# Expert lists of a routed MoE: rows of a table in memory, loaded for each step, in place of one-hot matmuls from the fourth expert on

## What is computed

```python
def hier_moe(h, w_rg, b_rg, w_re, b_re, w_gate, w_up, w_down):
    x = h.reshape(-1, D)
    gprob = softmax(x @ w_rg + b_rg)              # 4 groups, the best one is taken
    gp, gidx = top_k(gprob, 1)
    elog_sel = (x @ w_re + b_re), the 4 of the group
    ep, eidx = top_k(softmax(elog_sel), 2)        # 2 of its 4 experts
    ep = ep / sum(ep)
    weights = gp * ep
    # for each of the 16 experts, with c its weight for each token (0 for most):
    y = (silu(x @ wg) * (x @ wu)) @ wd            # 1024 -> 512 -> 1024
    acc = acc + c[:, None] * y
x = x + hier_moe(rmsnorm(x));  output rmsnorm(x)
```

## Time and profile before

| what | value |
|---|---|
| median of 3 runs | 881.52 us |
| the profiled execution | 881.83 us |
| its span | 880.0 us, so 1.8 us lie around it |
| TensorE busy | 846.6 us (96%) |
| VectorE, ScalarE, GpSimd busy | 525.6, 376.2, 251.2 us (60%, 43%, 29%) |
| experts (block 3) | from 431 us to the end |
| TensorE's clock in the steps | 1.00 of full speed |
| DMA in the steps | 0.79 to 0.94 of the 16 engines' time, about 300 GB/s |

### The profile page before, as it was taken

The page is one execution under the profiler, slowest core; times in us unless marked ns, Lnnn a source line. Parts: engine busy times, 40 slices in busy tenths (PEclk is TensorE's granted clock), DMA queues, the critical chain, the costliest instruction groups (busy, mean ns, idle before and its releaser), DMA issues.

```text
span 880.0 us, 15697 instructions
## 1 busy us (share of the span) xinstructions
PE 846.6 (96%) x5784; PEld 748.8 (85%) x5784; DVE 525.6 (60%) x1211; ACT 376.2 (43%) x710; POOL 251.2 (29%) x272
## 2 busy tenths in 40 slices
PE   4999999999999999999899999999999999999993
PEld 3999878999988887776699988899988999888892
DVE  5526424566778435456675576666666655765673
ACT  7445302645357524544335433344343454333542
POOL 1000000000000020001145655546554556453662
PEclk9999999999999899998599999999999999999997
DMA  9220101102222092436278889888799888899771
GB/s 297 59 96 10 39 1 48 49 1 56 49 96 96 13 294 74 177 140 226 70 249 302 291 292 355 279 307 299 282 317 335 296 290 283 286 365 308 257 252 58
DMA packets 117609, 167.08 MB, mean 190 GB/s; under 512 B 15988, under 2 KB 94904, under 8 KB 117573
## 3 DMA queue, kind: packets, MB, share of 16 engines
q1 hardware_dynamic: 102213, 136.00, 45.8%
q0 software_dynamic: 15360, 30.59, 10.1%
HBM read 147.36 MB, written 41.17 MB: 214 GB/s over the span
## 4 chain that ended last, share of the span: by engine, by line
PE 40%; POOL 3%; issue 3%; DVE 2%; DMA 1%; ACT 1%; POOLq 0%; DVEq 0%; ACTq 0%
PE bank L1891 26%; PE bank L1901 3%; PE bank L1912 3%; PE bank L1903 3%; PE bank L1902 3%; PE bank L1879 1%; DMA out<-ot,lists_now 1%; POOL out L1799 1%; POOL hold_at L1815 1%; PE bank L1872 1%; DVE wdlo L2095 1%; ACT split L1991 0%; POOL big L1786 0%; POOL sums L1799 0%; PE bank L1884 0%
## 5 line engine op out<-in xcount | busy, mean ns | idle before, releaser
L1891 PE MATMUL bank<-big,ring 128*128 128x160 f32 x2048 | 285.1, 300 | 1.4 <-DVE x L2167 1.3
L1891 PEld LDWEIGHTS bank<-big,ring 128*128 128x128 f32 x2048 | 280.8, 190 | 2.8 <-DVE x L2167 1.4
L1815 POOL TENSOR_TENSOR hold_at<-ident 128x1 f32<-128x1 f32 x63 | 55.1, 875 | 167.1 <-DVE lists L2062 120.7
L2095 DVE TENSOR_TENSOR wdlo<-wdn,split 128x1024 fp32r<-128x1024 f32 x64 | 76.7, 1218 | 0.0
L1991 ACT CAST split<-wdn 128x1024 fp32r<-128x1024 f32 x64 | 64.9, 1039 | 0.0
L1987 ACT ACTIVATE sg<-bank 128x160 f32<-128x160 f32 x64 | 19.4, 304 | 105.9 <-PE bank L1891 105.7
L499 PE MATMUL bank<-split,ring_r 128*128 128x384 f32 (+1 forms) x192 | 64.5, 336 | 0.1
L501 PE MATMUL bank<-split,ring_r 128*128 128x384 f32 (+1 forms) x192 | 61.7, 321 | 0.0
L1901 PE MATMUL bank<-split,hs 128*128 128x512 f32 x128 | 52.6, 411 | 0.0
L2090 DVE TENSOR_TENSOR hs<-hid,hs 128x128 fp32r<-128x128 f32 x64 | 18.8, 293 | 56.5 <-ACT hs L1993 56.5
L1378 PE MATMUL bank<-split,ring_r 128*128 128x512 f32 (+1 forms) x128 | 51.7, 404 | 0.3 <-PEq L1170 0.3
(11 more groups left out here) (386 smaller groups left out, 1821.2 us busy)
## 6 DMA issues: line engine op xcount, KB each, us to landing
wdn<-in_w_down SPq DMA_DIRECT2D x32, 1024.0 KB, 9.4
ring<-in_w_gate SPq DMA_DIRECT2D x32, 1024.0 KB, 6.0
ring<-in_w_up SPq DMA_DIRECT2D x32, 1024.0 KB, 9.5
ring<-in_w_in SPq DMA_DIRECT2D x8, 1024.0 KB, 6.2
x<-in_x_prompt SPq DMA_DIRECT2D x8, 512.0 KB, 5.9
h_rows<-h SPq DMA_DIRECT2D x8, 512.0 KB, 2.6
sums<-x SPq DMA_DIRECT2D x8, 512.0 KB, 3.7
v<-in_x_prompt SPq DMA_DIRECT2D x4, 512.0 KB, 6.9
```

The lines of the kernel that those rows point to most:

```text
L1815: nc.gpsimd.tensor_tensor(hold_at[:], ident[:, 0:1], ident[:, 1:2], ALU.add).then_inc(e_hold, 1)
L1891: x = nc.tensor.matmul(bank[f % 2][:, side * 256:side * 256 + W], ring[:, u, k, c0:c0 + P], xT[:, k, :], start=k == 0, stop=k == KC - 1)
L2095: nc.vector.tensor_tensor(wdlo[:, k, :], wdn[:, k // 2, (k % 2) * D:(k % 2 + 1) * D], wdhi[:, k, :].bitcast(F32), ALU.subtract).then_inc(e ...
```

## The change

From the fourth expert on the lists are no longer made by one-hot products. Block 3 works out, once, for each token and each of its two experts the row number in a table `records` in DRAM (18304 rows of 8 float32, 32 bytes; row = group start + rank), writes a record of the four list entries and the weight, and sends the records there with 18 indirect DMAs of 128 rows each. In each step SyncE loads the 160 rows of a later step's group with five DMAs, and three VectorE instructions make lists and weights of them. The lists of experts 0 to 2 are still made the old way. Block 2 fills the table with blank records first, and makes `table` for three experts only.

```diff
+        nc.gpsimd.memset(blank[:], 0.0).then_inc(r_gc, 1)
...
+        sp.wait_ge(r_gc, GC + 7)
+        sp.dma_start(places.records.rearrange("(p r) c -> p (r c)", p=P), blank[:].rearrange("p r c -> p (r c)")
+                     ).then_inc(s_states, 16)
...
         for part in (2, 3, 4):
-            link(nc.vector.tensor_copy(table[:, :, :, part], rest))
+            link(nc.vector.tensor_copy(table[:, 0:3, :, part], rest))
...
@@ SyncE, block 3, at the end of each loop pass
+            sp.wait_ge(e_sent, 16 * 2 * TT)
+            sp.wait_ge(e_idx, i + 3)
+            group_rows = places.records[0:GROUPS * W, :].rearrange("(s r) c -> s r c", r=W)[bass.ds(i + 3, 1), :, :]
+            sp.dma_start(listed[:, 0, :], group_rows[:, 0:P, :].rearrange("o r c -> (o r) c")).then_inc(e_list, 16)
+            for j in range(4):
+                sp.dma_start(listed[j * W2:(j + 1) * W2, 1, :], group_rows[:, P:W, :].rearrange("o r c -> (o r) c")
+                             ).then_inc(e_list, 16)
...
@@ GpSimd, block 3, between the first rows_old and the loop
+        pool.wait_ge(e_record, 1)
+        for a in range(2):
+            for t in range(TT):
+                nc.gpsimd.indirect_dma_start(
+                    out=places.records, in_=record[:, a, t, :], in_offset=None, bounds_check=GROUPS * W - 1,
+                    out_offset=bass.IndirectOffsetOnAxis(ap=row_at[:, a, t:t + 1], axis=0),
+                    oob_is_err=False).then_inc(e_sent, 16)
...
@@ TensorE, step
             if not last:
-                pe.wait_ge(e_oh, i + 3)
-                pe.wait_ge(e_idx, i + 2)
-                indices(facts)
+                if first:
+                    pe.wait_ge(e_oh, 3)
+                    pe.wait_ge(e_idx, 2)
+                    indices(table[:, 2, :, :])
                 pe.wait_ge(e_xg, i * 16 + 32)
...
@@ VectorE, block 3
+        def places_of():
+            ranks = rank_m[:].rearrange("p (e t) -> p t e", e=NE)
+            for a in range(2):
+                m = weighing.picks[:, a, :, :]
+                nc.vector.tensor_tensor(chosen[:, a, :, :], m, ranks, ALU.mult)
...
+        def records_of():
+            token = places.token[:].unsqueeze(1).broadcast_to([P, 2, TT])
+            link(nc.vector.tensor_tensor(second[:, 0, :], group[:, 3, :], group[:, 2, :], ALU.is_lt))
...
+        def next_list(i):
+
+            dve.wait_ge(e_list, i * 80)
+            nc.vector.tensor_copy(lists[:, :, 0], listed[:, 0, 0:4])
+            nc.vector.tensor_copy(weight[:], listed[:, :, 4])
+            nc.vector.scalar_tensor_tensor(out=lists[:, :, 1], in0=listed[:, 1, 0:4], scalar=4.0,
+                                           in1=chunk[:].broadcast_to([P, 4]), op0=ALU.mult, op1=ALU.add).then_inc(e_idx, 1)
+        places_of()
...
         def third_table():
-            dve.wait_ge(e_rk, 2)
             onehot(2)
-            dve.wait_ge(e_oh, 3)
-            lower(2)
+            records_of()
             dve.wait_ge(e_g, 80)
...
@@ VectorE, step
-                dve.wait_ge(e_ix, i + 3)
-                indices(i + 2)
-                dve.wait_ge(e_rk, i + 3)
-                onehot((i + 3) % NE)
-                dve.wait_ge(e_oh, i + 4)
-                lower((i + 3) % NE)
+                if first:
+                    dve.wait_ge(e_ix, 3)
+                    indices(2)
+                else:
+                    next_list(i)
```

More of the change, by code:

```diff
@@ L57 @@
 ROUNDS = -(-N // W)
+GROUPS = NE * ROUNDS + 2
+FIELDS = 8
+RUN = -(-GROUPS * W // P)
+OUTSIDE = float(1 << 18)
 class Weighing:
@@ L98, in state_products_out, with __init__ @@
     x.then_inc(signal, 1)
+class Places:
+    def __init__(self, sb, records):
+        self.start = sb("group_start", [P, NE])
+        self.limit = sb("round_limit", [P, ROUNDS - 1])
+        self.token = sb("token", [P, TT])
+        self.outside = sb("outside", [P, TT])
+        self.records = records
 class Halves:
@@ L134, in program @@
     sums_dram = nc.dram_tensor("sums", [N, D], F32).ap()
+    records = nc.dram_tensor("records", [RUN * P, FIELDS], F32).ap()
     with ExitStack() as whole:
@@ L188, in program @@
         lists0 = sb("lists0", [P, 2], I32)
+        places = Places(sb, records)
         s_w = [sem(f"s_w{j}") for j in range(5)]
@@ L1174, in b2_all @@
 def b2_all(nc, A, O, S0, Sp, s_w, samples, halves, sb, sem, e_w, wdn, bank, ident, onesf, eps_c, uT, gT, ring, x1, x_rows, h2_dram,
-           sums_dram, rank_m, table, iota_w, steps, once, weighing, rows_0):
+           sums_dram, rank_m, table, iota_w, steps, once, weighing, rows_0, places):
     c2 = ExitStack()
@@ L1196, in b2_all @@
     later = sb("later", [P, TT, 4], ctx=c2)
+    blank = sb("blank", [P, RUN, FIELDS], ctx=c2)
     both = sb("both", [P, TT, 4], ctx=c2)
@@ L1255, in _ @@
                        allow_small_or_imprecise_dtypes=True).then_inc(r_gc, 1)
+        nc.gpsimd.memset(blank[:], 0.0).then_inc(r_gc, 1)
+        nc.gpsimd.iota(places.start[:], [[W, NE]], base=0, channel_multiplier=0,
+                       allow_small_or_imprecise_dtypes=True).then_inc(r_gc, 1)
+        nc.gpsimd.iota(places.limit[:], [[W, ROUNDS - 1]], base=W, channel_multiplier=0,
+                       allow_small_or_imprecise_dtypes=True).then_inc(r_gc, 1)
+        nc.gpsimd.iota(places.token[:], [[P, TT]], base=0, channel_multiplier=1,
+                       allow_small_or_imprecise_dtypes=True).then_inc(r_gc, 1)
+        nc.gpsimd.memset(places.outside[:], 0.0).then_inc(r_gc, 1)
+        pool.wait_ge(r_gc, GC + 5)
+        nc.gpsimd.memset(blank[:, :, 1:4], FAR).then_inc(r_gc, 1)
+        pool.wait_ge(r_gc, GC + 6)
+        nc.gpsimd.memset(places.outside[NS:P, TT - 1:TT], OUTSIDE).then_inc(r_gc, 1)
+        pool.wait_ge(r_gc, GC + 7)
         for p in range(2):
@@ L1694, in b3_all @@
 def b3_all(nc, A, O, S0, samples, sb, sem, e_w, ring, wdn, bank, ident, eps_c, rows, h2_dram, sums_dram, rank_m, table, iota_w, steps,
-           once, weighing, rows_0):
+           once, weighing, rows_0, places):
     c3 = ExitStack()
     xg, xg2, xT, oh, wdhi, chunk = rows_0.xg, rows_0.xg2, rows_0.xT, rows_0.oh, rows_0.wdhi, rows_0.chunk
-    facts = sb("facts", [P, TT, PARTS], BF16, ctx=c3)
+    chosen = sb("chosen", [P, 4, TT, NE], ctx=c3)
+    group = sb("group", [P, 4, TT], ctx=c3)
+    past = sb("past", [P, 2, TT, ROUNDS - 1], ctx=c3)
+    row = sb("row", [P, 2, TT], ctx=c3)
+    row_at = sb("row_at", [P, 2, TT], I32, ctx=c3)
+    second = sb("second", [P, 2, TT], ctx=c3)
+    inside = sb("inside", [P, 2, TT], ctx=c3)
+    record = sb("record", [P, 2, TT, FIELDS], ctx=c3)
+    listed = sb("listed", [P, 2, FIELDS], ctx=c3)
     far = sb("far", [P, 2], ctx=c3)
@@ L1934, in step @@
                     pe.wait_ge(e_idx, 1)
-                    indices(facts)
+                    indices(table[:, 1, :, :])
                 if f == 0 and not first:
@@ L2068, in _, with link, picked @@
         dve.sem_inc(e_z, 1)
-        lower(0)
+        chain = [0]
+        def link(ins):
+            chain[0] += 1
+            ins.then_inc(e_d, 1)
+            dve.wait_ge(e_d, chain[0])
+        def picked(a, field):
+            return record[:, a, :, field]
+        def places_of():
[3 more added lines that the diff above has]
+                nc.vector.tensor_tensor(chosen[:, a, :, :], m, ranks, ALU.mult)
+                x = nc.vector.tensor_tensor(chosen[:, 2 + a, :, :], m, places.start[:].unsqueeze(1).broadcast_to([P, TT, NE]),
+                                            ALU.mult)
+            link(x)
+            link(nc.vector.tensor_reduce(group[:], chosen[:], axis=AX.X, op=ALU.add))
+            link(nc.vector.tensor_tensor(past[:], group[:, 0:2, :].unsqueeze(3).broadcast_to([P, 2, TT, ROUNDS - 1]),
+                                         places.limit[:].unsqueeze(1).unsqueeze(1).broadcast_to([P, 2, TT, ROUNDS - 1]),
+                                         ALU.is_ge))
+            link(nc.vector.tensor_reduce(row[:], past[:], axis=AX.X, op=ALU.add))
+            link(nc.vector.scalar_tensor_tensor(out=row[:], in0=row[:], scalar=float((NE - 1) * W), in1=group[:, 0:2, :],
+                                                op0=ALU.mult, op1=ALU.add))
+            link(nc.vector.tensor_tensor(row[:], row[:], group[:, 2:4, :], ALU.add))
+            link(nc.vector.tensor_tensor(row_at[:], row[:], places.outside[:].unsqueeze(1).broadcast_to([P, 2, TT]), ALU.add))
@@ L2101, in first_lists @@
             indices(0)
-            dve.wait_ge(e_rk, 1)
             onehot(1)
         def next_lists():
-            dve.wait_ge(e_oh, 2)
-            lower(1)
             dve.wait_ge(e_idx, 1)
```

40 lines of the change are left out of this document (25 added, 15 removed).

## The result

The changed kernel took **892.16 us** (median of 5 runs, 891.67 to 893.37) where the kernel before took 881.84 (5 runs, 879.96 to 883.59): a ratio of 1.0121, 95% interval 1.0105 to 1.0138. The prediction said 883.9, range 877.5 to 891.0. The sign was right, the size was not.

The account below looks back on a forecast made before the run. TensorE, 96% busy, was taken as the bound, with GpSimd's round close behind. 881.83 - 6.0 - 1.7 + 0.1 + 9.5 + 0.5 = 884.2, or 883.9 us as a median; range 877.5 to 891.

Parts of the forecast that it names:

- Parts 1 and 2: Steps: 14 sets of list matmuls leave TensorE, -6.0 us; VectorE and GpSimd relieved, one late step back to 26.84, -1.7 us.
- Part 1: TensorE's steps: 14 list matmul sets of 0.43 us go, -6.0 us; `hid` of the last quarter fits with 0.25 to spare.
- Part 3: Block 3's start and step 0: places_of, taken as 3 us, costs 0; records_of on VectorE costs +0.1 us, bounds 0 and 1.5.
- Part 4, the queue: GpSimd's queue: 18 scatters at 1.28 us, 23.0 us, plus some four low halves; last ends at about 477.3.
- Part 4, "Who waits": Steps 1 and 2: late rows of x and late e_free stall TensorE once, +9.5 us.
- both predicted waits: Step 1: TensorE idle 5 us for rows of step 2; VectorE waiting some 14 us for e_free.
- Part 4, SyncE "Nothing more": SyncE's wait for all scatters before step 2's lists and gate weights: weights land by 493, no further cost.
- Clock: TensorE's clock drops after its pauses, losses mostly hidden under the waits for z2 and `hid`: +0.5 us, bounds 0 and 2.
- Part 5: List loads, 256 pieces of 32 bytes a step: 0 on the path, up to 0.5 us a step if they push weights.
- Rival 2: DMA engines are the bound while scattering, 13 or 26 us of all engines; 887 to 892 us, chance 0.15.

Follow-up runs that it names:

- e1: The change without its 18 scatters and SyncE's wait for them, so lists from the fourth expert on are blank; 873.72 us.
- g1: The change with two GpSimd memsets, 1.9 us together, behind the sixth and behind the twelfth scatter; 891.1 us.
- i1: g1 with SyncE's list load, and its wait for all scatters, moved behind the first two weight loads of the step wanting the list; 888.32 us.
- i2: g2 with SyncE's list load back at the end of the step before; 880.83 us.
- g2: The change with places_of at the end of block 2, records_of at block 3's start, scatters in three idle GpSimd stretches, list load moved as in i1; 872.16 us.
- e4: The change with 18 gathers of the same 32-byte rows in place of the scatters; 891.32 us.
- f2: The change without scatters, but with 18 reads of 32-byte rows in a row behind GpSimd's first full round; 902.76 us.
- f1: The change with only the first six of its 18 scatters, the other twelve left out; 877.03 us.

## Why the prediction was right in sign and wrong in size

- **Parts 1 and 2** (-6.0 and -1.7, steps of 26.41): right. Of the 14 shortened steps 13 come after the disturbed one; they lasted 26.41 in the mean and gave -7.3, as the terms give for 13. That the mean hits 26.41 is in part luck: an undisturbed step lasts 26.33, so the 18 matmuls were worth 0.51, and in the steps of 26.4 to 26.5 TensorE waited for `hid` of the last quarter, whose slack of 0.25 us Part 1 counted as enough. In e1 all 14 gave -7.3, where the terms give -7.7.
- **Part 3** (+0.1): right. `places_of` took 3.2 us (3 predicted), step 0 ended 0.1 later.
- **Part 4, the queue**: right as far as it is GpSimd's own. 18 DMAs at 1.29 us, 475.4 for the last end where 477.3 was predicted (low halves lengthened two of them, where the sum allowed for four; VectorE took none from 460 to 481); 32-byte rows cost what rows of 4 KB cost.
- **Part 4, "Who waits"**: this is the step that failed. It let TensorE run on at full pace while GpSimd issued, and priced the loss at +9.5 by what comes late behind the queue; step 1 lost 17.4, in TensorE itself. What it describes did not happen in the change: VectorE found e_free in time, because it came late itself, and TensorE was not idle from 480 to 508 but slow from 460 to 481. Where the crawl was taken away with memsets (g1), both predicted waits appeared, at 5.1 and 16.8 us. So the late queue is real, and in the change a larger and earlier loss covered it.
- **The size of that term** can't be read from the change. In i1, with SyncE's wait out of the way and the last scatter 2.9 us later than predicted, steps 1 and 2 lost 12.6 where 9.5 + 0.5 stood in the sum. That is near, but made otherwise: 6.7 us of idle time and 5.8 of slower matmuls.
- **Part 4, SyncE "Nothing more"**: wrong. Without the long crawl the wait for the scatters in front of the weight loads is worth some 6 us of two steps (g1 against i1). In the spread version it may be part of the 4.5 us that steps 1 and 2 lost (i2 against g2). In the change the crawl hid this too.
- **Clock** (+0.5, bounds 0 and 2): too small, with the crawl and without it. The mean over step 1 was 0.81; the busy time of TensorE there was 7.2 us longer than in the next step, and in g1, without a crawl, 5.4 us longer over two steps. The prediction let the waits for z2 and `hid` hide the slow matmuls; the runs show them beside the idle time.
- **Part 5** (lists 0): the steady steps bear it out.
- **Rival 2** named 887 to 892 and the time came out at its end, for another reason. It had the DMA engines as the bound, with 13 us of each engine for the scatters, or 26; they stood at 0.03 of their time, and all 18 scatters took some 0.7 us of each engine. The rival's price of 91 ns was for packets of up to 4 KB; here a packet held eight records. It drew on the rule that the Trainium skill gives in DMA: Bandwidth & Descriptors, section Specifications, that pieces under 512 bytes are written by reading and writing back. No such cost shows in the trace: a scatter took 0.04 us of each engine, a read of the same rows (e4) 0.09. A time inside a rival's range is no evidence for the rival.
- **The range** reached 891.0, to a stall of some 17 by either of two known mechanisms. None of the rivals was "something that I have no row for". 18 indirect DMAs in a row is three times the longest row of before (two reads and four stores), and the price of one was taken as the price of all.

## What to carry to other kernels

When a change issues something many times in a row, look at how long a row the trace of before already shows; beyond that length the price of one says nothing about the rest. Put such a block where its engine is idle, in pieces no longer than the rows that already run, and move waits on it behind the loads that others need soon. And when a suspected cause is taken away and the time stays, look at the trace before dropping it: in g1 the crawl had gone, and a wait that it had covered stood in its place.

## What the runs showed of the hardware

- When GpSimd issued indirect DMAs with only 0.2 to 0.5 us between them, TensorE crawled from the eighth to tenth on, 9 to 12 us in, until the row and what directly followed it were issued: 21 us in the change, 28 in f2. It then handed out one to four matmuls and waited 0.3 to 2.4 us, with operands ready, and the matmuls that began again stood multiples of some 0.71 us apart (f2: 495.99, 496.70, 497.42, 498.13, 499.54, 500.96), while GpSimd kept its 1.29 us a DMA and the DMA engines were nearly idle (0.03).
- TensorE's signals came late with it, by 17 to 23 us in the eight long crawls. VectorE, ScalarE and SyncE stood still for want of these signals; once they came VectorE and ScalarE worked at their usual pace (f2, 517 to 521 us).
- It happened with writes and reads, with pieces of 32 and of 512 bytes, in a first pass of the loop and in a later one. Rows of six with 1.9 us of memsets between them had none (g1) or a short one (i1), rows of three with waits for landing had none; an addition of 0.2 us after each sixth did not help. Where the edge lies is not settled: f1, with ten DMAs, had a short one; g2 had 14 with pauses of 0.5 us and none; i2, with nearly the same row, a short one.
- What holds TensorE in it stays open: no run takes it apart further.
- The time of an indirect DMA of 128 rows on GpSimd was about 1 us (0.95 to 1.04) for rows of 32 bytes, of 512 bytes, of 1 KB and of 4 KB alike, where no large instruction of VectorE ran beside it.
